# First attention with the values as the stationary operand, two heads side by side in TensorE's column halves

## The chip, the core and the metric

The kernel runs on one core of a Trainium2 chip. The metric is the device time of one execution in microseconds (us). The core has a matmul engine (TensorE, PE in the views, with its weight loads shown as PEld), a vector engine (VectorE, DVE), a scalar engine (ScalarE, ACT), GpSimd (POOL) and a DMA queue that SyncE (SP) fills. Each engine works through its own instructions in order and waits on semaphores that others raise.

## The reference

One decoder layer on x (512 tokens x 1024). A single input projection feeds two attention branches. Cut to what matters here:

```
h = x @ w_in; split into qa, ka, va, ga, iq, ik, iw, c_q, c_kv, k_rope, gb
# branch A: 8 heads of 64; a token indexer picks 128 keys for each query
att = qa . ka * 64**-0.5, where the key is picked and causal, else -inf
o_a = softmax(att) @ va                      # per head
# branch B: 8 heads, latent attention, keys of 64 + 32, values of 64, causal
o_b = softmax(...) @ vb
out = concat(o_a * silu(ga), o_b * silu(gb)) @ w_out
x   = layernorm(2**0.25 * x + out)
```

## The kernel before

The 512 tokens are four row tiles of 128. After the input projections (until about 172 us of the profiled execution), both attentions run in one loop over **units**. A unit is one row tile and one head; there are 32 of branch A (units 0 to 31) and 32 of branch B (32 to 63). Row tiles come in the order 3, 2, 1, 0 (`ORDER`), so that a unit has N = 512, 384, 256 or 128 keys (up to the diagonal), eight heads of each in a row.

The loop is software-pipelined by numbers written out by hand. At **step u** TensorE issues the scores of unit u (`scores`, two f32r matmuls into one of two PSUM banks), the transposes of unit u-2 (`transposes`, `T_LAG`; one per 128 keys, into one of two PSUM slots) and the outputs of unit u-4 (`outputs`, `PV_LAG`). In between, VectorE masks the scores and takes their minimum (`mask_unit`), ScalarE exponentiates with a row sum (`exp_unit`), and ScalarE copies the transposed probabilities from PSUM to SBUF (`copy_probsT`, a ring of three buffers). The scores of unit u wait for the mask of u-2, the transposes wait for the exponentials and for the copy of the slot two before, and the outputs wait for the copy.

In branch A's outputs (line 1369) the transposed probabilities (128 keys x 128 queries) are loaded as weights and the values stream, 64 columns. These are plain-f32 matmuls, which the trace shows as two records each: 80 matmuls, 160 records. When a row tile is through, VectorE divides by the row sums (`normalise`, 128x512 out of PSUM) and multiplies by the gate (`apply_gate`); TensorE transposes the result in four pieces (`o_transposes(i, 0)`), ScalarE rounds it out of PSUM (`copy_oT_hi`) and VectorE takes the remainder (`oT_low`) for the output projection (`out_products`, line 1425), which is spread over the steps of branch B.

GpSimd has, in its queue, the rounding of w_out (`wo_hi`, `wo_lo`; the last eight pieces at line 528), two low parts of branch B's values (line 522), and in branch B the merging of pairs (`merge_pair`) and the scaling of gates (`scale_gate`, line 504).

Of the kernel before, what the change touches and what calls it, by code (L numbers as in the profile page):

```python
# [6 lines left out]
P = 128  # L7
# [13 lines left out]
BANK = 512  # L21
# [6 lines left out]
def build(nc, x, xT, positions, freqs, w_in, q_norm_g, w_uq, kv_norm_g, w_ukv, w_out, ln_g, ln_b, out):  # L28
# [60 lines left out]

    def unit(u):  # L90
        v, h = divmod(u, HEADS)
        m = ORDER[v % TT]
        return v, m, h, (m + 1) * P


    O_AFTER = [[NU_A + HEADS * (i + 1) + OT_AT - T_LAG + b for b in range(2)] for i in range(TT - 1)] + [[NU, NU]]
    O_AFTER[0][0] = O_FIRST
# [48 lines left out]
    o_norm = sb("o_norm", 92, [P, A_WIDTH])  # L146
# [29 lines left out]
    probsT = sb("probsT", 26, [P, 3, BANK])  # L176
# [31 lines left out]
    neg_max, row_sum, rinv = col(8), col(NU), col(HEADS)  # L208
    stats, aggr, rstd = col(24), col(3), col(1)
    minus_half, unused = col(2 * TT), col(1)  # L210

    with ExitStack() as ctx:
# [40 lines left out]
        transposed, probsT_copied = sem("transposed"), sem("probsT_copied")  # L253
# [5 lines left out]
        o_ps_read, o_ready = sem("o_ps_read"), sem("o_ready")  # L259
# [60 lines left out]

        def pair_done(g):

            return NU_A + 2 * (g + 1)
# [13 lines left out]
        def oT_low(eng, i, b):  # L337

            dst = (oT0, oT1)[i % 2]
            eng.wait_ge(oT_hi_ready, 2 * i + b + 1)  # L340
            src = ps_pT[:, slot_of[i, b] % 2].rearrange("p (a b) -> p a b", a=4) if b == 0 else obT[:, :, :]
            eng.tensor_tensor(dst[:, 1, 4 * b:4 * b + 4, :], src, dst[:, 0, 4 * b:4 * b + 4, :],
                              ALU.subtract).then_inc(oT_lo_ready, 1)
# [92 lines left out]
        def _(pool):  # L436
# [83 lines left out]
            for j in (3, 2):  # L520
# [3 lines left out]
            for j in range(KT, 2 * KT):  # L524
                k = j // 2
                pool.wait_ge(raw_b_loaded[k - KT // 2], 16)
                pool.wait_ge(wo_hi_ready, 2 * WO_ORDER.index(k) + 2)
                pool.tensor_tensor(wo_lo(k, j % 2), wo_raw_b[:, k - KT // 2, j % 2], wo_hi[:, k, j % 2],
                                   ALU.subtract).then_inc(w_lo_ready, 1)
# [6 lines left out]
            for g in range(POOL_PAIRS, NPAIR):  # L536
                if g > 0 and g % 4 == 0:
                    oT_low(pool, g // 4 - 1, 1)
                merge_pair(pool, g)
                if g == 1:  # L540
# [15 lines left out]
        def _(act):  # L556
# [124 lines left out]
            def exp_unit(u):  # L681
# [3 lines left out]
                               scale=-1.0, accum_out=row_sum[:, u:u + 1]).then_inc(probs_ready, 1)  # L685
# [12 lines left out]
            def copy_probsT(u):  # L698
                N = unit(u)[3]
                act.wait_ge(transposed, slot_of[u] + 1)  # L700
                if u >= 3:
                    act.wait_ge(pv_done, u - 2)
                dst = probsT[:, u % 3, 0:N] if u < NU_A else probsT_b[:, u % 3, 0, 0:N]
                act.activation(dst, ps_pT[:, slot_of[u] % 2, 0:N], ACT.Copy).then_inc(probsT_copied, 1)  # L704

            def copy_oT_hi(i, b):
                n = slot_of[i, b]
# [4 lines left out]
                if b == 0:  # L712
                    act.wait_ge(transposed, n + 1)
                    src = ps_pT[:, n % 2].rearrange("p (a b) -> p a b", a=4)
# [3 lines left out]
                act.activation((oT0, oT1)[i % 2][:, 0, 4 * b:4 * b + 4, :], src, ACT.Copy).then_inc(oT_hi_ready, 1)  # L718

# [19 lines left out]
            for u in range(NU + T_LAG):  # L739
                if u >= T_LAG:  # L740
# [9 lines left out]
                if u == O_FIRST + T_LAG:  # L750
                    copy_oT_hi(0, 0)
                if 0 < i < TT and j == OT_AT + 2:
# [15 lines left out]
        def _(dve):  # L768
# [188 lines left out]
            def normalise(v):  # L957

                dve.wait_ge(pv_done, HEADS * (v + 1))
                after(V.reciprocal(rinv, row_sum[:, HEADS * v:HEADS * (v + 1)]))  # L960
                V.tensor_tensor(o_norm[:, :].rearrange("p (h d) -> p h d", h=HEADS),
                                ps_o[:, v % 2].rearrange("p (h d) -> p h d", h=HEADS),
                                rinv.unsqueeze(2).broadcast_to([P, HEADS, A_DIM]), ALU.mult).then_inc(o_ps_read, 1)

            def apply_gate(v):
                m = ORDER[v % TT]
                cols = slice(A_WIDTH * (v // TT), A_WIDTH * (v // TT + 1))
                dve.wait_ge(o_ps_read, v + 1)
                wait_tok(dve, G_GA, m)
                V.tensor_tensor(gate[:, m, cols], o_norm[:, :], gate[:, m, cols], ALU.mult).then_inc(o_ready, 1)  # L970

            def probs_low(u):
                N, w = unit(u)[3], u % 3
                dve.wait_ge(probsT_copied, u + 1)
# [73 lines left out]
            for u in range(NU):  # L1048
                if u >= 2:
                    mask_unit(u)  # L1050
                if u - T_LAG >= NU_A:
# [6 lines left out]
                if 0 < v <= TT and j == PV_LAG and v != TT - 1:  # L1058
                    normalise(v - 1)
                if 0 < v <= TT and j == PV_LAG + 1 and v != TT - 1:  # L1060
                    apply_gate(v - 1)
                if u == NU_A:
                    normalise(TT - 2)
                if u == NU_A + 2:
                    apply_gate(TT - 2)
# [4 lines left out]
                if u == O_FIRST + T_LAG + 1:  # L1070
                    oT_low(V, 0, 0)
# [39 lines left out]
        def _(pe):  # L1111
# [223 lines left out]
            def slot(n):  # L1335
# [3 lines left out]
                elif not isinstance(slots[n - 2], int):  # L1339
                    i, b = slots[n - 2]  # L1340
                    pe.wait_ge(*((oT_lo_ready, 2 * i + 1), (obT_ready, i + 1))[b])
                elif slots[n - 2] < NU_A:
                    pe.wait_ge(probsT_copied, slots[n - 2] + 1)
# [12 lines left out]
            def outputs(u):  # L1356
                v, m, h, N = unit(u)
                if v < TT:
                    if h == 0:
                        if v < 2:  # L1360
                            pe.wait_ge(acc_read[v], ACC_LAST[v])
                        else:
                            pe.wait_ge(o_ps_read, v - 1)
                        if v == 0:
                            for t in range(TT):
                                wait_tok(pe, G_V, t)
                    pe.wait_ge(probsT_copied, u + 1)
# [144 lines left out]
```

## Time and profile before

| | us |
|---|---|
| median of 3 runs | 301.69 (301.47 to 302.53) |
| the profiled execution | 301.67 |
| its span in the trace | 299.9 |
| TensorE busy | 291.2 (97%) |
| VectorE, ScalarE, GpSimd busy | 228.5, 165.6, 169.8 |
| branch A's outputs (line 1369), 160 records | 21.4 busy |
| granted TensorE clock, mean | 0.992 |

What ends outside the span is 1.8 us. A line of the timeline is: start and length in us, engine, line, operation, output <- inputs, shapes, count, and in brackets the idle time of the engine before it with what ended it. Records of TensorE overlap, since matmuls are pipelined: what one costs its engine is read from the distance between starts, not from its length. The same holds, to a smaller degree, for VectorE and ScalarE. Line numbers are those of the kernel before.

### The profile page before, as it was taken

The numbers are of one execution on the slowest core, as the hardware profiler recorded it, in microseconds if no ns is written. First come the engines' busy times: TensorE is split into PE (matmuls) and PEld (weight loads), VectorE is DVE, ScalarE is ACT, GpSimd is POOL, SyncE is SP. The second block draws the span as 40 slices with busy tenths as digits, with TensorE's granted clock in tenths as the row PEclk, the third lists the DMA queues.
The fourth block names the chain that finished last, engine by engine and source line by source line (L and its number), as shares of the span: only waits on it lengthen the run. The fifth ranks groups of instructions, "written<-read, shape, count | busy, mean of one in ns | idle before, by whom it ended". The sixth has DMA issues, their size and how long they took to land.

```text
span 299.9 us, 5192 instructions
## 1 busy us (share of the span) xinstructions
PE 291.2 (97%) x1664; PEld 248.6 (83%) x1664; DVE 228.5 (76%) x523; ACT 165.6 (55%) x397; POOL 169.8 (57%) x197
## 2 busy tenths in 40 slices
PE   8999999999999999999999999999999999999990
PEld 7999987778888888888888789998677788888890
DVE  2898689879999999994134663564898878977785
ACT  4754533692252272383267787888877786553200
POOL 5798965106999975445317697630594161817211
PEclk9999999999999999999999999999999999999996
DMA  7965552200533723220056577301940000030412
GB/s 230 354 183 179 144 149 75 67 0 0 154 96 102 207 76 105 70 72 0 0 149 143 211 203 156 125 2 43 359 161 3 0 0 2 36 106 3 140 70 72
DMA packets 19547, 31.86 MB, mean 106 GB/s; under 512 B 6496, under 2 KB 9056, under 8 KB 19520
## 3 DMA queue, kind: packets, MB, share of 16 engines
q1 hardware_dynamic: 19088, 31.35, 34.4%
q8 instruction: 14, 0.23, 0.3%
q10 hardware_dynamic: 432, 0.18, 0.3%
q14 instruction: 13, 0.11, 0.1%
HBM read 26.28 MB, written 2.10 MB: 95 GB/s over the span
## 4 chain that ended last, share of the span: by engine, by line
PE 93%; DVE 2%; DMA 1%; ACT 1%; issue 1%; DVEq 0%; ACTq 0%
PE ps L1117 50%; PE ps L1425 15%; PE ps L1353 6%; PE ps L1318 5%; PE ps L1369 5%; PE ps L1384 3%; PE ps L1308 2%; PE ps L1132 2%; PE ps L1311 2%; PE ps L1221 1%; DMA w_raw<-in_w_in 1%; PE ps L1242 1%; PE ps L1398 1%; DVE y_last L1031 0%; ACT probs L684 0%
## 5 line engine op out<-in xcount | busy, mean ns | idle before, releaser
L474 POOL TENSOR_TENSOR w_lo<-w_raw,w_hi 128x512 fp32r<-128x512 f32 (+3 forms) x62 | 79.3, 1301 | 34.0 <-ACT w_hi L573 33.8
L1117 PE MATMUL ps<-w_hi,x_lo 128*128 128x512 f32 (+2 forms) x224 | 82.6, 372 | 0.0
L1117 PE MATMUL ps<-w_lo,x_hi 128*128 128x512 f32 (+2 forms) x224 | 82.5, 371 | 0.0
L573 ACT ACTIVATE w_hi<-w_raw 128x512 fp32r<-128x512 f32 (+3 forms) x62 | 35.9, 590 | 68.9 <-PE ps L1117 61.8
L1117 PE MATMUL ps<-w_hi,x_hi 128*128 128x512 f32 (+1 forms) x188 | 73.6, 391 | 0.0
L1117 PEld LDWEIGHTS ps<-w_hi,x_lo 128*128 128x128 f32 x224 | 42.1, 188 | 6.5
L1117 PEld LDWEIGHTS ps<-w_lo,x_hi 128*128 128x128 f32 x224 | 42.2, 188 | 6.0
L1425 PE MATMUL ps<-wo_hi,oT 128*128 128x512 f32 (+1 forms) x144 | 43.5, 372 | 0.0
L1117 PEld LDWEIGHTS ps<-w_hi,x_hi 128*128 128x128 f32 x188 | 35.3, 188 | 7.1 <-ACT w_hi L573 0.7
L684 ACT ACTIVATE probs<-probs,small 128x512 f32<-128x512 f32 (+3 forms) x64 | 35.8, 559 | 7.6 <-DVE small L944 7.0
L1353 PE MATMUL ps<-ident,probs 128*128 128x128 f32 x160 | 28.3, 274 | 0.4 <-ACT probs L684 0.2
L1425 PEld LDWEIGHTS ps<-wo_hi,oT 128*128 128x128 f32 x144 | 25.7, 189 | 3.3
L1353 PEld LDWEIGHTS ps<-ident,probs 128*128 128x128 f32 x160 | 20.1, 140 | 9.5 <-issue 5.2
L332 POOL TENSOR_TENSOR obT<-half_sum,crossed 64x128 f32<-64x128 f32 x30 | 15.7, 522 | 17.8 <-ACT crossed L737 16.1
L901 DVE MATCH_REPLACE8 score<-small,score 128x256 f32<-128x256 f32 (+2 forms) x48 | 25.7, 554 | 0.0
L944 DVE CUSTOM_DVE_ANT_0 probs<-ps,score 128x512 f32<-128x512 f32 (+2 forms) x24 | 13.3, 556 | 15.1 <-PE ps L1311 15.1
L898 DVE MAX8 small<-score 128x8 f32<-128x256 f32 (+2 forms) x48 | 23.7, 556 | 0.0
L944 DVE CUSTOM_DVE_ANT_0 probs<-ps,causal 128x128 f32<-128x128 f32 (+3 forms) x40 | 17.8, 444 | 7.0 <-PE ps L1318 3.4
L1318 PE MATMUL ps<-kbT,qbT 96*128 96x512 f32 (+3 forms) x64 | 22.7, 435 | 0.0
L1369 PE MATMUL ps<-va,probsT 128*128 128x64 f32 x160 | 21.4, 264 | 0.0
L1369 PEld LDWEIGHTS ps<-va,probsT 128*128 128x128 f32 x160 | 20.5, 193 | 0.6 <-issue 0.6
L975 DVE TENSOR_TENSOR probsT_b<-ps,probsT_b 128x512 fp32r<-128x512 f32 (+3 forms) x32 | 15.6, 488 | 5.0 <-ACT probsT_b L704 4.7
(164 smaller groups left out, 548.5 us busy)
## 6 DMA issues: line engine op xcount, KB each, us to landing
w_raw<-in_w_in SPq DMA_DIRECT2D x20, 512.0 KB, 3.7
kaT_swap<-kaT SPq DMA_DIRECT2D x8, 256.0 KB, 3.7
w_raw<-in_w_out SPq DMA_DIRECT2D x4, 512.0 KB, 4.9
wo_early<-in_w_out SPq DMA_DIRECT2D x4, 512.0 KB, 5.3
wo_raw_b<-in_w_out SPq DMA_DIRECT2D x4, 512.0 KB, 5.6
x_res<-in_x SPq DMA_DIRECT2D x4, 512.0 KB, 6.6
x_raw<-in_xT SPq DMA_DIRECT2D x3, 512.0 KB, 6.9
out_y<-y SPq DMA_DIRECT2D x6, 256.0 KB, 2.1
```

The source lines that it names most:

```text
L332: eng.tensor_tensor(obT[rows, g % 4], half_sum[rows, g % 2, a], crossed[rows, g % 2], ALU.add).then_inc(pair_merged, 1)
L474: pool.tensor_tensor(w_lo[:, s, 0:n], w_raw[:, s, 0:n], w_hi[:, s, 0:n], ALU.subtract).then_inc(w_lo_ready, 1)
L573: act.activation(dst, w_raw[:, s, 0:n], ACT.Copy).then_inc(w_hi_ready, 1)
L684: act.activation(probs[:, u % NPROBS, 0:N], probs[:, u % NPROBS, 0:N], ACT.Exp, bias=neg_max[:, u % 8:u % 8 + 1], scale=-1.0, accum_out=ro ...
L898: step(V.max(top8[:, 8 * j:8 * j + 8], sc))
L901: step(V.match_replace(out=sc, in_to_replace=top8[:, 8 * j:8 * j + 8], in_values=sc, imm_value=TAKEN))
L944: V.tensor_tensor_reduce(out=probs[:, u % NPROBS, 0:N], in0=ps_s[:, u % 2, 0:N], in1=bias, scale=-scale, scalar=3.0e38, op0=ALU.add, op1=A ...
L1117: ins = mm(dst, a, b, start=start and j == 0, stop=stop and j == len(pairs) - 1)
L1318: ins = mm(ps_s[:, b, 0:N], qbT[:, h, t], kbT[:, h, 0:N], start=True, stop=True)
L1353: ins = nc.tensor.transpose(bank[:, j * P:(j + 1) * P], probs[:, u % NPROBS, j * P:(j + 1) * P], ident[:, :])
L1369: ins = mm(ps_o[:, v % 2, h * A_DIM:(h + 1) * A_DIM], probsT[:, u % 3, j * P:(j + 1) * P], va[:, j, h * A_DIM:(h + 1) * A_DIM], start=(j = ...
L1425: ins = mm(out_ps(i, b), oT[i % 2][:, o, k, :], w[:, wcols], start=first, stop=final)
```

## The change

Branch A's loop is changed in six ways; branch B's arithmetic stays.

1. **Order of units.** The row tiles of branch A come in two blocks, (3, 0) and (2, 1): `unit(u)` takes two heads of the long tile, two heads of the short tile, two more of the long, and so on. Key counts run 512, 512, 128, 128 four times, then 384, 384, 256, 256 four times.
2. **Outputs.** The values (128 keys x 64) are the weights, and the transposed probabilities stream, 128 columns. The even head of a pair writes PSUM partitions 0 to 63, the odd one 64 to 127. TensorE does them four units at a visit, at steps 7, 11, ... 35. The result stands transposed, heads on partitions, in four banks instead of two.
3. **Copies.** VectorE makes three of four copies of branch A's transposed probabilities, ScalarE the fourth (`by_dve`); the ring has five buffers.
4. **Gates.** GpSimd scales a tile's gate by the reciprocal row sums (`scale_gate_a`), TensorE transposes the gate instead of the result (after units 26, 28, 34 and 36), ScalarE copies it out (`turn_gate`) and VectorE multiplies (`gate_oaT`). `normalise` and `apply_gate` are gone.
5. **Output projection.** Its first half for row tile 3 begins at step 41 with three matmuls a step (before: step 34, two a step). The rounded copies of branch A's result come out of SBUF.
6. **GpSimd's queue** takes the first `oT_low` and the four gates, and two of the four late w_out pieces move behind merges of branch B.

```diff
+    BLOCKS = [(0, 3), (1, 2)]
     def unit(u):
-        v, h = divmod(u, HEADS)
+        if u < NU_A:
+            n, r = divmod(u, BLOCK_UNITS)
+            v, h = BLOCKS[n][r % 4 // 2], r // 4 * 2 + r % 2
...
+        def by_dve(u):
+            return u < NU_A and u % 4 != ACT_COPY
...
+        def copy_free(eng, u):
+            if u < NU_A:
+                if u >= len(probsT):
+                    eng.wait_ge(pv_done, u + 1 - len(probsT))
...
+            for v in BLOCKS[0]:
+                scale_gate_a(v)
+            vb_low_pool(3)
+            oT_low(pool, 0, 0)
+            vb_low_pool(2)
+            for v in BLOCKS[1]:
+                scale_gate_a(v)
+            for k in range(KT // 2, KT - 2):
+                wo_low_b(k)
...
+            def gate_oaT(v):
+                half = gate[:, ORDER[v], 0:A_WIDTH]
+                dve.wait_ge(gate_a_turned, A_RANK.index(v) + 1)
+                dve.wait_ge(pv_done, BLOCK_UNITS * (A_RANK.index(v) // 2 + 1))
+                V.tensor_tensor(half, oa_bank(v), half, ALU.mult).then_inc(o_ps_read, 1)
...
-                        ins = mm(ps_o[:, v % 2, h * A_DIM:(h + 1) * A_DIM], probsT[:, u % 3, j * P:(j + 1) * P],
-                                 va[:, j, h * A_DIM:(h + 1) * A_DIM], start=(j == 0), stop=(j == m))
+                    for w in (u - 3, u - 1):
...
+                        for j in range(m + 1):
+                            for a in range(2):
+                                ins = mm(oa_bank(v)[A_DIM * a:A_DIM * (a + 1), h // 2 * P:(h // 2 + 1) * P],
+                                         va[:, j, (h + a) * A_DIM:(h + a + 1) * A_DIM],
+                                         probsT[(w + a) % len(probsT)][:, j * P:(j + 1) * P], start=(j == 0), stop=(j == m))
...
-O_FIRST = 16
-A_HALF_AT = 34
+O_FIRST = 33
+TURN_AT = [26, 34, 36, 28]
+ACT_COPY = 3
+A_HALF_AT = 41
```

**TensorE, inside branch A.** The kernel before, one step of a unit with 512 keys (kaT and qaT are keys and queries, ident the identity of the transposes, va the values):

```order
L1308 MATMUL ps<-kaT,qaT 128x512 [waits masked_ready]
L1311 MATMUL ps<-kaT_swap,qaT 128x512
L1353 MATMUL ps<-ident,probs 128x128 [waits probs_ready,probsT_copied]
L1353 MATMUL ps<-ident,probs 128x128 x3
L1369 MATMUL ps<-va,probsT 128x64 [waits probsT_copied]
L1369 MATMUL ps<-va,probsT 128x64 x3
```

The kernel after, from the second long unit of a group (step 9) to the beginning of the visit (step 11):

```order
L1384 MATMUL ps<-kaT_swap,qaT 128x512
L1426 MATMUL ps<-ident,probs 128x128 [waits probs_ready,probsT_copied_dve]
L1381 MATMUL ps<-kaT,qaT 128x128 [waits masked_ready]
L1384 MATMUL ps<-kaT_swap,qaT 128x128
L1426 MATMUL ps<-ident,probs 128x128 [waits probs_ready,probsT_copied_dve]
L1426 MATMUL ps<-ident,probs 128x128 x3
L1381 MATMUL ps<-kaT,qaT 128x128 [waits masked_ready]
L1384 MATMUL ps<-kaT_swap,qaT 128x128
L1426 MATMUL ps<-ident,probs 128x128 [waits probs_ready,probsT_copied]
L1426 MATMUL ps<-ident,probs 128x128 x3
L1447 MATMUL ps<-probsT_105,va 64x128 [waits probsT_copied_dve]
L1447 MATMUL ps<-probsT_101,va 64x128
```

Between the scores of a unit and its transposes there stood two steps' outputs; now there stand only scores and transposes, and the outputs of four units (ten matmuls, two heads in turn) come in one piece behind the fourth step.

**VectorE, inside branch A.** The kernel before, around the end of the first row tile (`ISA` rows are the masks and the reads of their minimum):

```order
L944 ISA probs,small<-ps,score 128x384 [waits transposed,scores_ready]
L944 ISA small 128x1
L960 RECIPROCAL small<-small 128x8 [waits pv_done]
L961 TENSOR_TENSOR o_norm<-ps,small 128x512 [waits dve_step]
L944 ISA probs,small<-ps,score 128x384 [waits transposed,scores_ready]
L944 ISA small 128x1
L970 TENSOR_TENSOR gate<-o_norm,gate 128x512 [waits acc_read3,o_ps_read]
```

The kernel after, steps 12 to 15:

```order
L1017 ISA probs,small<-ps,score 128x512 [waits transposed,scores_ready]
L1017 ISA small 128x1
L1032 COPY probsT_101<-ps 128x128 [waits pv_done,transposed]
L1017 ISA probs,small<-ps,score 128x512 [waits transposed,scores_ready]
L1017 ISA small 128x1
L1017 ISA probs,small<-ps,causal 128x128 [waits transposed,scores_ready]
L1017 ISA small 128x1
L1032 COPY probsT_103<-ps 128x512 [waits pv_done,transposed]
L1017 ISA probs,small<-ps,causal 128x128 [waits transposed,scores_ready]
L1017 ISA small 128x1
L1032 COPY probsT_104<-ps 128x512 [waits pv_done,transposed]
```

The two wide operations for each row tile are gone from between the masks, and a copy stands behind three of four masks.

**GpSimd, around the end of branch A.** The kernel before, from its last early piece of w_out on (vb_parts are branch B's values, wo_lo_b the late pieces, obT the merged pairs):

```order
L519 TENSOR_TENSOR wo_lo_a<-w_raw,wo_hi 128x512
L522 TENSOR_TENSOR vb_parts_98<-vb,vb_parts_98 128x4x128 [waits vb_hi_ready]
L522 TENSOR_TENSOR vb_parts_97<-vb,vb_parts_97 128x4x128 [waits vb_hi_ready]
L528 TENSOR_TENSOR wo_lo_b<-wo_raw_b,wo_hi 128x512 [waits wo_hi_ready,raw_b_loaded0] x2
L528 TENSOR_TENSOR wo_lo_b<-wo_raw_b,wo_hi 128x512 [waits wo_hi_ready,raw_b_loaded1] x2
```

The kernel after:

```order
L563 TENSOR_TENSOR wo_lo_a<-w_raw,wo_hi 128x512
L571 TENSOR_TENSOR gate<-gate,small 128x512 [waits acc_read3,rinv_a_ready]
L571 TENSOR_TENSOR gate<-gate,small 128x512 [waits acc_read0,rinv_a_ready]
L576 TENSOR_TENSOR vb_parts_97<-vb,vb_parts_97 128x4x128 [waits vb_hi_ready]
L386 TENSOR_TENSOR oT_68<-gate,oT_68 128x512 [waits oT_hi_ready]
L576 TENSOR_TENSOR vb_parts_96<-vb,vb_parts_96 128x4x128 [waits vb_hi_ready]
L571 TENSOR_TENSOR gate<-gate,small 128x512 [waits acc_read2,rinv_a_ready]
L571 TENSOR_TENSOR gate<-gate,small 128x512 [waits acc_read1,rinv_a_ready]
L584 TENSOR_TENSOR wo_lo_b<-wo_raw_b,wo_hi 128x512 [waits wo_hi_ready,raw_b_loaded0]
```

Four gates and one `oT_low` have come in; the second values piece, for which branch B's first outputs wait, stands behind the `oT_low`, and that waits for ScalarE's copy at step 33.

## Rows read from the trace of the kernel before

**Rows 1.** Windows view: us, busy PE, PEld, DVE, ACT, POOL (instructions), clock, DMA share, GB/s.
```profile
core 0 of [0], span 299.9 us
...
172.00:208.00 36.00, 35.76 (x296) 33.99 (x295) 19.22 (x71) 29.92 (x92) 21.01 (x25) 1.00 0.38 101
```

**Rows 2.** TensorE in time (start, length in us): one unit of 512 keys.
```profile
175.86 0.48 PE L1308 MATMUL ps<-kaT,qaT 128*128 128x512 f32 x1
...
176.41 0.60 PE L1353 MATMUL ps<-ident,probs 128*128 128x128 f32 x4
...
176.85 1.00 PE L1369 MATMUL ps<-va,probsT 128*128 128x64 f32 x8
...
177.66 0.48 PE L1308 MATMUL ps<-kaT,qaT 128*128 128x512 f32 x1
```

**Rows 3.** TensorE in time: starts of units with 384, 256 and 128 keys.
```profile
191.81 0.42 PE L1308 MATMUL ps<-kaT,qaT 128*128 128x384 f32 x1
...
193.17 0.36 PE L1308 MATMUL ps<-kaT,qaT 128*128 128x256 f32 x1
...
199.52 0.36 PE L1308 MATMUL ps<-kaT,qaT 128*128 128x256 f32 x1
...
200.42 0.37 PE L1308 MATMUL ps<-kaT,qaT 128*128 128x256 f32 x1
...
206.03 0.31 PE L1308 MATMUL ps<-kaT,qaT 128*128 128x128 f32 x1
...
206.57 0.30 PE L1308 MATMUL ps<-kaT,qaT 128*128 128x128 f32 x1
```

**Rows 4.** TensorE in time: plain-f32 scores of second attention, then transposes.
```profile
216.65 1.02 PE L1318 MATMUL ps<-kbT,qbT 96*128 96x512 f32 x2
...
217.51 0.60 PE L1353 MATMUL ps<-ident,probs 128*128 128x128 f32 x4
```

**Rows 5.** TensorE in time: matmuls in four strips of 32 rows.
```profile
59.99 0.50 PE L1221 MATMUL ps<-ik_hi,iq_hi 32*128 32x512 f32 x4
...
60.56 0.40 PE L1221 MATMUL ps<-ik_hi,iq_lo 32*128 32x512 f32 x4
...
60.89 0.50 PE L1117 MATMUL ps<-w_hi,x_hi 128*128 128x512 f32 x1
```

**Rows 6.** Timeline: from unit 2's scores to its transposes, four engines.
```profile
172.05 0.39 PE L1308 MATMUL ps<-kaT,qaT 128*128 128x512 f32 x1
...
172.71 0.69 DVE L944 CUSTOM_DVE_ANT_0 probs<-ps,score 128x512 f32<-128x512 f32 x1 [2.45 <-PE ps L1311]
...
173.64 0.71 ACT L684 ACTIVATE probs<-probs,small 128x512 f32<-128x512 f32 x1
...
174.56 0.42 PEld L1353 LDWEIGHTS ps<-ident,probs 128*128 128x128 f32 x4 [0.52 <-issue]
```

**Rows 7.** VectorE in time: a mask of 512 keys and the operation behind it.
```profile
220.42 0.68 DVE L944 CUSTOM_DVE_ANT_0 probs<-ps,causal 128x512 f32<-128x512 f32 x1
221.03 0.08 DVE L944 DVE_READ_ACCUMULATOR2_ANT small<- 128x1 f32 x1
```

**Rows 8.** Groups by line and shape (busy us, mean ns | idle before).
```profile
L1369 PEld LDWEIGHTS ps<-va,probsT 128*128 128x128 f32 x160 | 20.5, 193 | 0.6 <-issue 0.6
...
L684 ACT ACTIVATE probs<-probs,small 128x384 f32<-128x384 f32 x16 | 9.8, 610 | 1.1 <-DVE small L944 1.0
...
L944 DVE CUSTOM_DVE_ANT_0 probs<-ps,causal 128x128 f32<-128x128 f32 x16 | 4.6, 286 | 4.0 <-PE ps L1311 3.3 <-PE ps L1318 0.5
```

**Rows 9.** GpSimd in time: pieces of its queue around the second attention.
```profile
213.24 1.29 POOL L522 TENSOR_TENSOR vb_parts<-vb,vb_parts 128x512 fp32r<-128x512 f32 x1 [11.03 <-ACT vb_parts L728]
...
214.49 10.93 POOL L528 TENSOR_TENSOR wo_lo_b<-wo_raw_b,wo_hi 128x512 fp32r<-128x512 f32 x8
...
230.01 1.05 POOL L504 TENSOR_TENSOR gate<-gate,small 128x512 f32<-128x512 f32 x1 [0.88 <-POOL obT L332]
```

**Rows 10.** Weight loads in time: a wait inside the first attention.
```profile
198.87 0.20 PEld L1353 LDWEIGHTS ps<-ident,probs 128*128 128x128 f32 x2 [0.31 <-DVE oT L342]
```

More of the change, by code:

```diff
@@ L88, in build, with sum_col @@
     NPAIR = TT * B_HEADS // 2
+    BLOCKS = [(0, 3), (1, 2)]
+    A_RANK = [v for block in BLOCKS for v in block]
+    BLOCK_UNITS = 2 * HEADS
     def unit(u):
-        v, h = divmod(u, HEADS)
+        if u < NU_A:
+            n, r = divmod(u, BLOCK_UNITS)
+            v, h = BLOCKS[n][r % 4 // 2], r // 4 * 2 + r % 2
+        else:
+            v, h = divmod(u, HEADS)
         m = ORDER[v % TT]
         return v, m, h, (m + 1) * P
-    O_AFTER = [[NU_A + HEADS * (i + 1) + OT_AT - T_LAG + b for b in range(2)] for i in range(TT - 1)] + [[NU, NU]]
-    O_AFTER[0][0] = O_FIRST
+    def sum_col(u):
+        v, m, h, N = unit(u)
+        return HEADS * (A_RANK.index(v) if v < TT else v) + h
+    O_AFTER = [[TURN_AT[i], NU_A + HEADS * (i + 1) + OT_AT - T_LAG + 1 if i < TT - 1 else NU] for i in range(TT)]
     slots = []
@@ L319, in out_ps, with wait_copied, oaT, oa_bank @@
             return bank[:, 0:PIECES[i][b].stop - PIECES[i][b].start]
+        def by_dve(u):
+            return u < NU_A and u % 4 != ACT_COPY
+        def wait_copied(eng, u):
+            n = sum(by_dve(w) for w in range(u + 1))
+            if by_dve(u):
+                eng.wait_ge(probsT_copied_dve, n)
+            else:
+                eng.wait_ge(probsT_copied, u + 1 - n)
+        def copy_free(eng, u):
+            if u < NU_A:
+                if u >= len(probsT):
+                    eng.wait_ge(pv_done, u + 1 - len(probsT))
+                return probsT[u % len(probsT)][:, 0:unit(u)[3]]
+            if u >= NU_A + 3:
+                eng.wait_ge(pv_done, u - 2)
+            return probsT_b[:, u % 3, 0, 0:unit(u)[3]]
+        def oaT(i):
+            return gate[:, ORDER[i], 0:A_WIDTH].rearrange("p (a b) -> p a b", a=4)
+        def oa_bank(v):
+            return (ps_o, ps_y)[A_RANK.index(v) // 2][:, A_RANK.index(v) % 2]
         def pair_done(g):
@@ L340, in oT_low @@
             eng.wait_ge(oT_hi_ready, 2 * i + b + 1)
-            src = ps_pT[:, slot_of[i, b] % 2].rearrange("p (a b) -> p a b", a=4) if b == 0 else obT[:, :, :]
+            src = oaT(i) if b == 0 else obT[:, :, :]
             eng.tensor_tensor(dst[:, 1, 4 * b:4 * b + 4, :], src, dst[:, 0, 4 * b:4 * b + 4, :],
@@ L539, in _ @@
                 merge_pair(pool, g)
+                if g <= 2:
+                    wo_low_b(KT - 3 + g)
                 if g == 1:
@@ L739, in _ @@
             for u in range(NU + T_LAG):
-                if u >= T_LAG:
+                if u >= T_LAG and not by_dve(u - T_LAG):
                     copy_probsT(u - T_LAG)
@@ L1050, in _ @@
                     mask_unit(u)
+                if u >= T_LAG and by_dve(u - T_LAG):
+                    copy_probsT(u - T_LAG)
                 if u - T_LAG >= NU_A:
@@ L1057, in _ @@
                 i = v - TT
[L1058 to L1065, printed above, removed]
+                if u in (BLOCK_UNITS + 2, NU_A + 2):
+                    row_sums_a(u // BLOCK_UNITS - 1)
+                if u - T_LAG - 2 in TURN_AT:
+                    gate_oaT(TURN_AT.index(u - T_LAG - 2))
                 if v > TT and j == 2:
@@ L1439, in _ @@
                 i, j = divmod(u - NU_A, HEADS)
[L1440 to L1445 removed]
+                for t in range(TT):
+                    if u == O_AFTER[t][0] + T_LAG:
+                        o_transposes(t, 0)
+                if 0 < i < TT and j == OT_AT + 1:
+                    o_transposes(i - 1, 1)
+                if 0 <= u - A_HALF_AT < 8:
+                    out_products(0, 3 * (u - A_HALF_AT), 3 * (u - A_HALF_AT + 1))
                 if 0 <= u - OUT_AT[0] - 2 < 6:
@@ L1452, in _ @@
             out_products(TT - 2, done, NSTEP - LAST_STEPS)
-            for b in range(2):
-                o_transposes(TT - 1, b)
+            o_transposes(TT - 1, 1)
             out_products(TT - 2, NSTEP - LAST_STEPS, NSTEP)
```

109 lines of the change are left out of this document (55 added, 54 removed).

## Prediction

> **What bounds the kernel now.** I read the windows view first. In the stretch of branch A, 172 to 208 us, TensorE is busy 35.76 of 36.00 us, VectorE 19.2, ScalarE 29.9, GpSimd 21.0 [rows 1]. So the matmuls set the pace, and what leaves TensorE there shortens the run, as long as nothing else comes up behind it. Next the timeline of TensorE. A unit of 512 keys takes 1.80 us: 0.55 from the first score matmul to the transposes, 0.44 for four transposes (0.11 each), 0.81 for eight records of outputs, 0.10 each [rows 2]. Units of 384, 256 and 128 keys take 1.36, 0.90 and 0.54 [rows 3]; less 0.11 for each transpose and 0.10 for each output record, that leaves 0.43, 0.28 and 0.23 for their scores. All 160 output records cost 16.1 us. The third thing to read is latency, at the one place where the trace shows it bare. Units 2 and 3 run before any outputs: scores at 172.05, mask at 172.71, exponentials at 173.64, transposes only at 174.56, and TensorE sat there ("issue", 0.52) [rows 6]. From scores to transposes are 2.5 us, against two steps of 1.8 us with outputs. **The outputs that the change shortens are what covers this chain.**
>
> **Part 1, the outputs.** A record now streams 128 columns. The nearest price is the plain-f32 scores of branch B: two records of 512 columns take 0.86 us, 0.107 for 128 columns [rows 4]. A visit has 20 records, in both blocks (4+1 or 3+2 key tiles, two heads, two records). If the halves overlap fully, a visit is 10 x 0.107 and one more stream until the second half is through, 1.18; if they don't, 20 x 0.107 = 2.14. That matmuls in separate parts of the array run together the trace shows for strips of rows only: three groups of four matmuls with 512 columns (the rows have the first and the third) take their turns from 59.99 to 60.89, 0.075 us each, where even 128 columns need 0.107 alone [rows 4, 5]. Leaving the strips cost at most 0.1: 0.33 from the last group to the next matmul, where the groups stand 0.285 apart [rows 5]. Behind the outputs the change to f32r matmuls costs 0.1 already today (below) and stands inside the 0.55. I take 1.2 for a visit, bounds 1.1 and 1.4. Eight visits are 9.6 us against 16.1: **-6.5**, bounds -7.3 and -4.9.
>
> The Trainium skill, "TensorEngine Tiling (Array Packing)", Key Properties, says that a change of tiling mode drains TensorE. With the 0.1 of rows 5 on either side a visit would be 1.4, which is the upper bound, and the sum 1.6 us worse; no run here shows it for columns yet.
>
> **Part 2, the chain.** One visit of the first block in steady state, from the moment t = 0 at which the scores of the long unit a begin. Constants: a result of TensorE is seen 0.20 after its last matmul's turn (172.05 to 172.71, and 0.10 more behind outputs, make 0.75 to the mask) [rows 2, 6]. A mask of 512 occupies VectorE for 0.61 [rows 7], one of 128 for about 0.22 (286 ns less the same overlap) [rows 8]; exponentials begin 0.73 after the mask (its 0.69 and a hand-over of 0.04, my estimate), occupy 0.71, and transposes come 0.95 after their start (0.92 to the weight load) [rows 6]. A copy by VectorE I take like a mask. TensorE:
> scores a 0 to 0.55, a short unit's transpose to 0.66, scores b to 1.21, a transpose to 1.32. Scores c wait until mask a is through and read, 0.75 + 0.61 + 0.13 = 1.49, and end at 1.72. Transposes of a: mask 0.75, exponentials 1.48, so 2.43; **wait 0.71**; end 2.87. Scores d to 3.10. Transposes of b: VectorE has mask a until 1.36, the copy of a short unit until 1.58, then mask b; exponentials at 2.38 (ScalarE has a until 2.19 and one copy), so 3.33; wait 0.23; end 3.77. Visit: 4.97. The old kernel needs 2 x 1.80 + 2 x 0.54 = 4.68 for the same units. The waits are 0.17 + 0.71 + 0.23 = **1.1**.
>
> The second block the same way, with 0.43, 0.28, masks 0.48 and 0.35 (between the two known), exponentials 0.61 [rows 8] and so transposes 0.85 after their start: scores c need no wait; a's transposes at 0.63 + 0.60 + 0.85 = 2.08 against 1.58, wait 0.5; b's wait 0.2. Together **0.7**.
>
> Sum of waits over the stage: the first group (steps 4 to 7) I take at 2.0, twice a steady one, since VectorE also has four transposes of branch B's queries there; two groups of the first block 2.2; three groups of the second 2.1; the last group has two gate transposes (4 x 0.11 each) in its holes, 0. That is 6.3. The old kernel has 0.52 and 0.31 of its own [rows 6, 10]. **Net +5.5**, bounds +3.5 and +7 (a tenth more or less in the hand-over in each link).
>
> **Part 3, what moves without much cost.** Sixteen gate transposes replace sixteen result transposes: nothing. VectorE loses 8 wide operations and gains 24 copies, 4 `gate_oaT` and 2 small reciprocals: per group of the first block masks 1.66 and copies 1.42, 3.1 us of 4.97, so it isn't the bound; what it costs is in the chain. ScalarE loses 24 copies and gains four. Three gate transposes leave places amid f32r matmuls, where each cost a change of kind, 3 x 0.1: **-0.3**. The output matmuls that move from steps 34-40 to 41-48 keep their number; the steps that they leave have TensorE work of some 1.8 us (0.86 + 0.44 + outputs), and VectorE about as much.
>
> **Part 4, GpSimd's queue.** At step 36 TensorE needs the second values piece for branch B's first outputs and the scaled gate of tile 2. Both stand behind the new `oT_low`, which waits for ScalarE's copy at step 33: from there 1.3 (the piece, and `oT_low` alike) + 1.29 + 1.05 = 3.6 us [rows 9]. By the steps' sizes TensorE gets there 3.1 to 3.6 us after that copy, so it waits up to 0.6, and 0.3 at the transposes of step 35, whose exponentials stand behind two value copies. I take **+0.7**, bounds 0 and +2. SyncE's loads of w_out are released by the scores of step 31, at nearly the same time.
>
> **Sum.** -6.5 + 5.5 - 0.3 + 0.7 = -0.6 us on the profiled execution's 301.67, which is the median's 301.69 to within 0.02: **301.1 us**. Its own range, with a visit and the chain at their bounds but not all at once, is 298.5 to 303.5.
>
> **Rivals.**
> *The chain doesn't bind.* If masks and exponentials come earlier than in my walk, the whole saving stays: -6.5 - 0.3 = -6.8, 294.9. For it: TensorE showed under 1 us of waits in 36 us. Against it: rows 6 show the 2.5 us bare, and steps without outputs are exactly what the change makes.
> *The column halves don't overlap.* Place: the visit. Price: 2.14 and two changes of mode, 2.3 instead of 1.2, 8 x 1.1 = +8.8: 309.9, slower. It decides from the point where a visit takes more than about 1.3 us. For it: no row shows column halves. Against it: rows 5, for strips of rows.
> The Trainium skill, "TensorE: Matmul & The Clock Gate", The mechanism, says that weight loads overlap matmuls in flight only when the row groups differ, and column halves share all rows. Taken at its word a visit would be near 4 us and the run 20 us slower. The trace disagrees for the whole array: output records 0.10 apart have loads of 0.19 on the same rows [rows 2, 8]. So I give it little of this rival's chance.
> *GpSimd is late for good.* Two late pieces of w_out (10.93 / 4 = 2.7 each) stand between merges of pairs, and behind the merges are VectorE's pair reads and the gating of `obT`. If its queue reaches branch B some 5 us late, TensorE waits at step 46 for one piece and a gate, 2.7 + 1.05 [rows 9]: +3.8 on the forecast, 304.9. Against it: it idled 11 us before the second values piece.
>
> **Chances.** Forecast 0.58 (of it faster by over half a per cent 0.22, within 0.30, slower 0.06); chain doesn't bind 0.16, all faster; halves don't overlap 0.14, slower; GpSimd late 0.12 (0.03 within, 0.09 slower). Half a per cent, 1.5 us, is about what a measurement can tell from no change. So faster 0.38, same 0.33, slower 0.29. The range, 294.0 to 306.5, leaves out the non-overlapping halves and about a third of the first rival.
>
> **What the profile after would show.** The visit: ten output matmuls in about 1.2 us; 2.1 or more refutes overlap. The chain: TensorE waiting in the first block about 0.7 before a's transposes, released by the exponentials, and VectorE near 60% in the stage; no wait there refutes the walk. GpSimd: the wait at step 36, and none at 46. The stage should still end near 208 us. I would be wrong above all if the waits come out at half or double.

## The result

| | us |
|---|---|
| before, median of 4 runs | 301.88 (301.47 to 302.53) |
| after, median of 4 runs | 308.16 (307.93 to 309.57) |
| ratio of the two | 1.0216, 95% interval 1.018 to 1.0252 |
| forecast | 301.1 (294.0 to 306.5) |

The changed kernel is slower, by 6.3 us, and outside the range. The profiled execution of after was the slowest of the four. A second profile of the same kernel, taken in the experiments, gave 307.81, so the comparison of places uses that one; the difference between the two profiles comes at the end. The busy times come first, from the page of that second profile:

```profile
PE 289.5 (95%) x1664; PEld 240.6 (79%) x1664; DVE 234.3 (77%) x540; ACT 157.7 (52%) x377; POOL 173.4 (57%) x202
```

TensorE's records cover 1.7 us less than before (289.5 against 291.2), while the span grew by 6.1 (306.0 against 299.9), so it isn't work that was added. These are TensorE's own waits from 172 us on, by what ended them, in the second profile of after (us in total, times, longest):

```profile
PE ps L1426 <- ACT probs L752: 3.8, 9, 0.6
PE ps L1426 <- ACT gate L789: 3.4, 3, 1.6
PE ps L1381 <- DVE small L1017: 0.6, 1, 0.6
PE ps L1478 <- POOL gate L571: 0.2, 1, 0.2
```

The kernel before has one wait of 0.2 us in this list; its two bare places inside branch A, 0.5 and 0.3, show in the weight loads [rows 6, 10]. Now three sorts of waits stand in it: for the exponentials (line 752), which the prediction walked; once for a mask (line 1381); and **3.4 us for ScalarE's copies of transposed gates (line 789)**, which it did not have at all. The 0.2 for a scaled gate (line 571) was forecast. Over 172 to 208 us the stage reads so now, against 35.76 busy before [rows 1]:

```profile
172.00:208.00 36.00, 30.05 (x257) 23.27 (x255) 24.34 (x84) 20.47 (x69) 22.34 (x27) 1.00 0.38 102
```

A steady group of the first block on TensorE, from the scores of one long unit to those of the next group. Read the starts; the idle time is in brackets:

```profile
184.56 0.51 PE L1381 MATMUL ps<-kaT,qaT 128*128 128x512 f32 x1
...
185.16 0.47 PE L1381 MATMUL ps<-kaT,qaT 128*128 128x512 f32 x1
...
186.09 0.33 PE L1381 MATMUL ps<-kaT,qaT 128*128 128x128 f32 x1
...
187.03 0.63 PE L1426 MATMUL ps<-ident,probs 128*128 128x128 f32 x4 [0.50 <-ACT probs L752]
...
187.90 0.63 PE L1426 MATMUL ps<-ident,probs 128*128 128x128 f32 x4
188.46 1.31 PE L1447 MATMUL ps<-probsT,va 128*64 128x128 f32 x20
189.70 0.45 PE L1381 MATMUL ps<-kaT,qaT 128*128 128x384 f32 x1
```

Up to the visit it is the walk of Part 2 to a few hundredths. From the first scores at 184.56 the scores of the short unit come at 1.53 (walked: 1.49), a's transposes at 2.47 with a wait of 0.50 (2.43, 0.71), b's at 3.34 (3.33). Then the visit: it was to begin at 3.77 and begins at 3.90, and it takes 1.24 us for its 20 records, so that the group is 5.14 long against 4.97 forecast. The halves do overlap: 0.062 us a record, against 0.107 for 128 columns alone [rows 4].

And this is the mechanism that the prediction missed, in time, on TensorE, VectorE and ScalarE (gate L1478 is the transpose of a gate, L789 its copy out of PSUM):

```profile
204.79 0.60 PE L1478 MATMUL ps<-ident,gate 128*128 128x128 f32 x4
...
206.13 0.28 PE L1384 MATMUL ps<-kaT_swap,qaT 128*128 128x256 f32 x1
...
206.26 0.08 DVE L1017 DVE_READ_ACCUMULATOR2_ANT small<- 128x1 f32 x1
...
206.49 0.61 ACT L752 ACTIVATE probs<-probs,small 128x384 f32<-128x384 f32 x1
...
207.08 0.59 ACT L789 ACTIVATE gate<-ps 128x512 f32<-128x512 f32 x1
...
207.72 0.55 PE L1426 MATMUL ps<-ident,probs 128*128 128x128 f32 x3 [1.31 <-ACT gate L789]
```

TensorE transposes the first gate at 204.79. Transposed probabilities and transposed gates share two PSUM slots, and the transposes of the unit two places later (unit 28, line 1426) need the gate's slot. ScalarE copies it out only at 207.08, since `turn_gate` stands in its queue one step later, behind the exponential of unit 29 (206.49), whose mask VectorE had read only at 206.34. TensorE is through with its scores of unit 30 (from 206.13) and stands for 1.31 us. The same happens twice more in branch B, where the list of waits has otherwise only 0.28 us for an exponential and 0.19 for a scaled gate:

```profile
223.43 0.66 PE L1426 MATMUL ps<-ident,probs 128*128 128x128 f32 x4 [0.54 <-ACT gate L789]
...
228.98 0.66 PE L1426 MATMUL ps<-ident,probs 128*128 128x128 f32 x4 [1.55 <-ACT gate L789]
```

### The profile page after: what moved, and what is told of

Same layout as the page of the kernel before. It is cut to its first block, busy times and chain, and to the rows that moved or that the text cites. A ratio compares the mean times of both kernels' runs of the same rounds, so it can differ in the third digit from the quotient of the medians.

```text
span 307.7 us, 5205 instructions
## 1 busy us (share of the span) xinstructions
PE 291.2 (95%) x1664; PEld 241.8 (79%) x1664; DVE 233.6 (76%) x540; ACT 157.8 (51%) x377; POOL 174.1 (57%) x202
## 4 chain that ended last, share of the span: by engine, by line
PE 89%; ACT 4%; issue 3%; DVE 2%; POOL 1%; DVEq 0%; POOLq 0%; ACTq 0%
PE ps L1190 49%; PE ps L1505 14%; PE ps L1426 6%; PE ps L1391 4%; PE ps L1447 3%; PE ps L1464 3%; PE ps L1205 2%; ACT probs L752 2%; PE ps L1336 1%; PE ps L1294 1%; PE ps L1478 1%; PE ps L1381 1%; PE ps L1315 1%; PE ps L1384 1%; ACT gate L789 0%
## 5 line engine op out<-in xcount | busy, mean ns | idle before, releaser
L1426 PE MATMUL ps<-ident,probs 128*128 128x128 f32 x160 | 29.2, 281 | 7.4 <-ACT probs L752 3.7
L1032 DVE COPY probsT<-ps 128x512 f32<-128x512 f32 (+3 forms) x24 | 12.8, 534 | 11.9 <-PE ps L1447 8.1
L770 ACT ACTIVATE probsT_b<-ps 128x512 fp32r<-128x512 f32 (+3 forms) x32 | 13.8, 430 | 14.1 <-PE ps L1426 14.0
L1464 PE MATMUL ps<-probsT_b,vb_parts 128*128 128x256 f32 x80 | 17.2, 312 | 0.0
```

The lines of the kernel that those rows point to most:

```text
L1426: ins = nc.tensor.transpose(bank[:, j * P:(j + 1) * P], probs[:, u % NPROBS, j * P:(j + 1) * P], ident[:, :])
L1464: ins = mm(ps_o[:, g % 2, 2 * P * a:2 * P * (a + 1)], vb_parts[j][:, h // 2, 2 * a:2 * a + 2].rearrange("p a d -> p (a d)"), probsT_b[:, u ...
```

## The experiments

Ratios refer to the kernel before, run on the same chip (301.8 to 302.0 us in each series). Differences to "after" refer to its median of 308.16, which comes from another series and is known to about 1.1 us either way (the interval of its ratio), so differences of less than that between such gains say little. Theory A: the late gate copies hold a transpose slot, and this costs about 3.4 us. Theory B: the bare chain of mask, exponential and transposes costs the rest, and a visit placed where it covers the chain gets it back. The rival: one of them is only the visible end of the other, so that undoing it exposes the other and the gain is shared.

### Gate copies one step earlier

```diff
-                if u - T_LAG - 1 in TURN_AT:
-                    turn_gate(TURN_AT.index(u - T_LAG - 1))
+                if u - T_LAG in TURN_AT:
+                    turn_gate(TURN_AT.index(u - T_LAG))
```

> Only ScalarE's queue is changed: the copy of a transposed gate stands one step earlier, behind the exponentials of step 28, 30, 36, 38 instead of 29, 31, 37, 39. Theory A (the gate's PSUM slot is held until ScalarE has copied it, and that copy stands behind an exponential that waits for a mask): the waits of 1.31, 0.54 and 1.55 us that end with that copy in the trace go, 3.4 us, 304.8. Rival (the transposes there would wait for their exponentials anyway): under 1 us, 307.2 or more.

Measured: 304.05 us (303.74 to 304.85), ratio 1.0086 (1.0065 to 1.0106). One place in ScalarE's queue is worth 4.1 us, give or take the 1.1 of after. Its waits:

```profile
PE ps L1426 <- ACT probs L752: 3.7, 9, 0.6
...
PE ps L1426 <- ACT gate L789: 0.2, 1, 0.2
```

3.4 us of gate waits have become 0.2, and the exponentials' waits, 3.8 before, are 3.7: they did not take the place of the others. The rows account for 3.2 of the 4.1. Theory A stands.

### The visit ahead of the next group's short scores

```diff
             for u in range(NU + PV_LAG):
+                if u % 4 == 2 and 6 <= u <= NU_A + 2:
+                    outputs(u - 3)
                 if 2 <= u < NU:
                     scores(u)
...
-                if u - PV_LAG >= 0:
+                if u - PV_LAG >= NU_A:
                     outputs(u - PV_LAG)
```

> The visit of four units' outputs stands ahead of the scores of the short unit c (step 4k+2) instead of behind the transposes of step 4k+3; nothing else. Theory B (TensorE waits in each group because nothing covers the chain from scores to transposes, and the visit can cover it): a group of the first block falls from 5.13 to about 4.0 us, one of the second from 4.57 to about 3.9, so 6 to 7 us over the stage, 301.5. Rival (VectorE or ScalarE is the bound in the stage, so that the place of the visit doesn't matter): groups stay near 5.1 and 4.6, under 1 us.

Measured: 304.55 us (304.14 to 306.04), ratio 1.0094 (1.0073 to 1.0115): 3.6 us faster than after, 3.1 short of what theory B gave. The gate copies were not touched and still cost 2.7 us of waits. What is new is 1.7 us of waits for ScalarE's copy of probabilities, which the next run shows in time.

### Both

> Both edits. If the two kinds of wait are separate, the gains add: 298.1 by theories A and B. If they share a chain, it is nearer to 300.5.

Measured: 301.94 us (301.44 to 302.76), ratio 1.0007 (0.9995 to 1.0019), as fast as the kernel before, and slower than both expectations: A and B together fall short. The waits for exponentials and masks are gone from the matmuls' list; in their place stands one line, which had 1.7 us in the run before:

```profile
PE ps L1447 <- ACT probsT L770: 2.6, 5, 0.9
```

```profile
184.69 1.09 PE L1447 MATMUL ps<-probsT,va 128*64 128x128 f32 x16
186.13 0.44 PE L1447 MATMUL ps<-probsT,va 128*64 128x128 f32 x4 [0.35 <-ACT probsT L770]
186.50 0.33 PE L1381 MATMUL ps<-kaT,qaT 128*128 128x128 f32 x1
```

The long pair's 16 records begin at 184.69, and the 4 of the short pair wait until 186.13 for ScalarE's copy of the fourth unit (line 770), which that engine makes behind an exponential. The next scores stand behind them. The visit was brought forward to cover a wait and ran into its own input. The separate gains, 4.1 and 3.6, make 7.7, and both edits together give 6.2. The 1.5 that is missing is hardly more than the noise of after, but 0.9 of it shows in the trace: with the gate waits gone, the wait for ScalarE's copy grows from 1.7 to 2.6. With the whole visit in this place part of the gain is shared, as the rival has it.

### The two heads of a pair one after the other

```diff
-                        for j in range(m + 1):
-                            for a in range(2):
+                        for a in range(2):
+                            for j in range(m + 1):
```

> The changed kernel with the two heads of a pair one after the other (all key tiles of the even head, then of the odd one) in place of in turn. If the two column halves overlap only where neighbours in the queue are in different halves, a visit goes from 1.24 us to 20 x 0.107 = 2.1, and the run by 8 x 0.9 = 7 us, 315. If the 1.24 us came from smaller weights alone, nothing changes.

Measured: 312.02 us (one run). A visit of the first block (4 + 1 key tiles) and one of the second (3 + 2):

```profile
185.26 1.80 PE L1447 MATMUL ps<-probsT,va 128*64 128x128 f32 x20
186.99 0.50 PE L1381 MATMUL ps<-kaT,qaT 128*128 128x512 f32 x1
...
201.60 1.58 PE L1447 MATMUL ps<-probsT,va 128*64 128x128 f32 x20
203.12 0.44 PE L1381 MATMUL ps<-kaT,qaT 128*128 128x384 f32 x1
```

Three visits take 1.73 us and four take 1.51, instead of 1.24 or 1.25, so these seven cost 2.5 us more. The first visit took 3.24 us, at a lowered clock (last column but two):

```profile
178.00:180.00 2.00, 2.00 (x16) 1.93 (x16) 0.26 (x3) 0.49 (x2) 2.00 (x3) 0.52 0.80 283
180.00:182.00 2.00, 2.00 (x14) 1.54 (x11) 0.69 (x1) 0.00 (x0) 1.92 (x3) 0.63 1.14 269
```

The only run of this kernel is thus to be set beside the execution of after that has the same (309.57, see the last experiment), and is 2.5 us slower than it, not the 3.9 that after's median gives; with one execution of each this is a rough figure. So the alternation of halves does make them overlap, but the heads one after the other are still below 20 x 0.107 = 2.14 us, and the loss is under half of the one expected. Matmuls at the joints between heads still have neighbours in the other half; since both kinds of visit have three joints and take 1.73 and 1.51, joints alone don't explain it. Why the rest overlaps stays open.

### The visit cut in two

Against the run of both edits; `outputs` has got the second argument:

```diff
                 if u % 4 == 2 and 6 <= u <= NU_A + 2:
-                    outputs(u - 3)
+                    outputs(u - 3, (0,))
                 if 2 <= u < NU:
                     scores(u)
                 if 0 <= u - T_LAG < NU:
                     transposes(u - T_LAG)
+                if u % 4 == 2 and 6 <= u <= NU_A + 2:
+                    outputs(u - 3, (1,))
```

Here (0,) is the long pair and (1,) the short one; the gate copies are a step earlier too.

> Both moves again (gate copies one step earlier on ScalarE, outputs of a group brought forward), but the visit is cut in two: the long pair stands ahead of the scores of step 4k+2 as before, the short pair behind the transposes of that step, so that the scores of a unit of the next group no longer queue behind ScalarE's copy of the last short unit. Theory C (with both moves in, what is left is the visit's wait for that copy: five waits for it, 2.6 us together, in the run of both moves): those waits go and about 2.5 us are won, 299.4 us, faster than the kernel before. Rival D (VectorE's turn of mask and copy bounds the group: ten waits of 0.3 us for its copies, each before transposes): the waits for ScalarE's copy are only exchanged for longer waits for VectorE's, less than 0.8 us is won, 301.2 us or more.

Measured: **298.88 us (298.63 to 298.94), ratio 0.9899 (0.9884 to 0.9913)**. It beats both kernels: 1.0% under the one before, 9.3 us under the changed one. All that is left in the list of the matmuls' waits, and the stage:

```profile
PE ps L1478 <- POOL gate L571: 0.2, 1, 0.2
```

```profile
172.00:208.00 36.00, 35.71 (x307) 26.82 (x306) 28.65 (x96) 24.00 (x77) 22.40 (x27) 1.00 0.45 125
```

35.71 us busy of 36: TensorE sets the pace again [rows 1]. A group of the first block, on TensorE:

```profile
178.04 0.48 PE L1381 MATMUL ps<-kaT,qaT 128*128 128x512 f32 x1
...
179.37 1.09 PE L1447 MATMUL ps<-probsT,va 128*64 128x128 f32 x16
180.39 0.33 PE L1381 MATMUL ps<-kaT,qaT 128*128 128x128 f32 x1
...
180.67 0.62 PE L1426 MATMUL ps<-ident,probs 128*128 128x128 f32 x4
181.22 0.44 PE L1447 MATMUL ps<-probsT,va 128*64 128x128 f32 x4
181.59 0.33 PE L1381 MATMUL ps<-kaT,qaT 128*128 128x128 f32 x1
...
182.25 0.48 PE L1381 MATMUL ps<-kaT,qaT 128*128 128x512 f32 x1
```

4.21 us (178.04 to 182.25) against 5.14 in after and 4.68 for the same units before. The long pair takes 1.02 us, the short one 0.37, together 0.15 more than a whole visit. Theory C held: the waits for ScalarE's copy are gone, and 3.1 us were won.

Of rival D something is left, where the list of matmul waits doesn't show it. A group of the second block, matmuls and weight loads:

```profile
190.50 0.42 PE L1381 MATMUL ps<-kaT,qaT 128*128 128x384 f32 x1
...
191.06 0.42 PE L1381 MATMUL ps<-kaT,qaT 128*128 128x384 f32 x1
...
191.63 0.20 PEld L1426 LDWEIGHTS ps<-ident,probs 128*128 128x128 f32 x2 [0.29 <-DVE probsT L1032]
...
192.08 0.66 PEld L1447 LDWEIGHTS ps<-probsT,va 128*64 128x64 f32 x12 [0.25 <-issue]
192.11 0.88 PE L1447 MATMUL ps<-probsT,va 128*64 128x128 f32 x12
192.91 0.39 PE L1381 MATMUL ps<-kaT,qaT 128*128 128x256 f32 x1
...
193.68 0.66 PE L1447 MATMUL ps<-probsT,va 128*64 128x128 f32 x8
...
194.27 0.39 PE L1381 MATMUL ps<-kaT,qaT 128*128 128x256 f32 x1
```

The weight loads stand 0.29 us for VectorE's copy, and the step from 191.06 to 192.11 takes 1.05 us for work that the prediction's prices put at 0.65. The ends of matmul records are modelled, so a short wait can hide between them. This group takes 4.36 us (to 194.86) and the next one 4.26, against 4.52 for the same units before. So the second block gains about 0.2 us a group, the first 0.5.

The parts of visits also show what a visit is made of: 4, 8, 12 and 16 records take 0.37, 0.59, 0.80 and 1.02 us and a whole visit of 20 takes 1.24, which is 0.15 and 0.054 for each record.

### The cut visit without the earlier gate copies

The edits of the visit stay; ScalarE's queue is the changed kernel's again.

```diff
-                if u - T_LAG in TURN_AT:
-                    turn_gate(TURN_AT.index(u - T_LAG))
+                if u - T_LAG - 1 in TURN_AT:
+                    turn_gate(TURN_AT.index(u - T_LAG - 1))
```

> The outputs brought forward and cut in two as in e7_split, but the gate copies left one step later on ScalarE, as in the changed kernel. Theory A (a gate transpose holds one of two transpose slots until ScalarE's copy, and this price is paid wherever the visits stand): the waits for the gate copies are back at steps 28, 38 and 40, and the time is 298.9 + 4 = 302.9 us. If the gate copies only cost while the chain of mask and exponential is bare as well, one of the three waits goes and the time is 300.5 us.

Measured: 302.18 us (301.89 to 302.99), ratio 1.0012 (1.0003 to 1.0022).

```profile
PE ps L1426 <- ACT gate L789: 2.9, 4, 1.6
```

With the chain covered the gate waits are all there, four of them now, 2.9 us, and the run costs 3.3 us more than with the copies a step earlier. So the four runs form a square: after 308.16, gate copies alone -4.1, cut visit alone -6.0, both -9.3. The 0.8 us by which the sum of the two differs from both together is within the noise of after, so with the cut visit the two causes are independent as far as these runs can tell, and the rival (one hides the other) falls for it. With the whole visit, above, part of the gain was shared.

### The whole visit behind the transposes, or between scores and transposes

Both with the earlier gate copies; `outputs(u - 3)` stands at step 4k+2, in the first run behind `transposes` (below), in the second between `scores` and `transposes`.

```diff
                 if 0 <= u - T_LAG < NU:
                     transposes(u - T_LAG)
-                if u - PV_LAG >= 0:
+                if u % 4 == 2 and 6 <= u <= NU_A + 2:
+                    outputs(u - 3)
+                if u - PV_LAG >= NU_A:
                     outputs(u - PV_LAG)
```

> Gate copies one step earlier, and the whole visit of four heads moved from step 4k+3 to step 4k+2, but behind the transposes of that step, so nothing covers the time from the first unit's mask to its transposes. If what the forward move of the visit won came from covering that chain, the wait of 0.5 us before the first long unit's transposes stays in each group and the time is near that of the earlier gate copies alone, 304.0 us. If it came from the visit lying a step earlier at all (copies released earlier), it is near 302.0 us.

Measured: 302.54 us (301.94 to 303.04), ratio 1.0021 (1.0012 to 1.0031), between the two expectations and nearer to the second.

```profile
PE ps L1426 <- ACT probs L752: 2.5, 6, 0.5
PE ps L1381 <- DVE small L1017: 1.1, 3, 0.6
```

> Gate copies one step earlier; the visit whole again, between the scores and the transposes of step 4k+2. By the rows of e7_split its two parts take TensorE 1.02 + 0.37 us against 1.24 for a whole visit, so one visit saves 0.15 x 8 = 1.2 us of work. Against that the scores of the short unit lose the long pair that stood ahead of them and wait for VectorE's mask of the first long unit (0.23 us in a steady group, 0.61 in the first, as in e9_behind), some 0.4 us a group with the copy of the last short unit: 8 x 0.4 - 1.2 = +2, 300.9 us. Rival: the visit covers whatever follows it, so that the place before or behind these scores doesn't matter, and the saved work is all gain: 297.7 us.

Measured: 300.63 us (300.17 to 301.19), ratio 0.996 (0.9947 to 0.9972), 0.3 from what was expected.

```profile
PE ps L1381 <- DVE small L1017: 1.2, 3, 0.6
```

Behind the transposes the visit covers nothing of the chain, and 2.5 us of waits for exponentials stay, though a step's advance alone won 1.5 us (the wait of 0.63 us at unit 21, below, is gone there). So of the 5.2 us between the gate copies alone and the cut visit (304.05 to 298.88), 1.5 come from the advance and only the other 3.7 from where within the step the outputs stand: theory B holds for the larger part. Between scores and transposes those waits are gone and the wait for the mask stays, 1.2 us in matmuls. Only ahead of both, with the part that isn't ready left for later, the matmuls have none of these waits.

### The changed kernel again

> The changed kernel unaltered, a second profile. If the 2.3 us of the first visit (178.7 to 181.0 us, at a granted clock of 0.5) is a matter of that one execution, the visit takes 1.25 us here, the span is 1.5 us shorter, 306.2, and the gate waits at steps 28, 38 and 40 (1.3, 0.5 and 1.5 us) are all there again. If short waits of TensorE lower the clock each time, the row with 0.5 is there again and the span is 307.7.

Measured: 307.81 us, span 306.0. The clock (last column but two) in the first profile of after, then in the second:

```profile
178.00:180.00 2.00, 2.00 (x16) 1.67 (x16) 0.45 (x3) 0.49 (x2) 2.00 (x3) 0.50 0.95 307
180.00:182.00 2.00, 2.00 (x17) 1.50 (x14) 0.88 (x2) 0.00 (x0) 1.92 (x4) 0.75 1.09 280
```

```profile
178.00:180.00 2.00, 2.00 (x25) 1.52 (x24) 1.00 (x4) 0.49 (x2) 2.00 (x3) 1.00 0.94 289
180.00:182.00 2.00, 1.39 (x8) 0.88 (x7) 1.79 (x8) 1.06 (x4) 1.92 (x3) 1.00 1.10 279
```

The granted clock was 0.50 for 2 us, that is the lower of its two levels, and 0.75 as a mean of the next 2, in one execution and full in the other, with waits of the same length ahead of it (0.61, 0.50 and 0.35 us). The first visit took 2.33 us at the lowered clock. The run of the two heads one after the other has the same waits and fell too (0.52 and 0.63), the run of the gate copies alone has them and did not; both ran on the same chip. The two profiles of after are 0.1 us apart at 172.3 us and 1.6 at the end of that visit, so the clock explains 1.5 of the 1.7 us of span between them, and nothing of the 6.3 between the kernels' medians.

## Where the prediction went wrong

By its own steps, against the second profile of after (span 306.0, before 299.9: +6.1, forecast -0.6).

- **Part 2, the walk: right.** 5.14 against 4.97, the waits in the forecast places. VectorE's share in the stage (24.34 of 36 us, 68%) came out above the 60% I named, and it is still not the bound.
- **Part 2, the last group, "two gate transposes in its holes, 0": wrong, and the main failure.** The gate transposes have a price that isn't TensorE's time: they hold a slot until another engine's queue gets to them. I followed them on TensorE alone, and in Part 3 set them equal to the old result transposes ("nothing"). The cost is 1.31 us at unit 28, and 0.54 and 1.55 in branch B at steps 38 and 40, where I had looked for no waits: **3.4 us in rows, 4.1 by the experiment**, which is the same within after's noise. For ScalarE I had only counted copies ("loses 24 copies and gains four"); behind what in its queue each of the four stands I did not ask.
- **Part 1, the visit: overlap right, size low.** A visit takes 1.24 us, but before its first weight load and before the first one behind it the loads stand still for 0.17 each:

```profile
183.32 1.07 PEld L1447 LDWEIGHTS ps<-probsT,va 128*64 128x64 f32 x20 [0.17 <-DVE probsT L1032]
184.56 0.19 PEld L1381 LDWEIGHTS ps<-kaT,qaT 128*128 128x128 f32 x1 [0.17 <-issue]
```

  The second stop lies within the 1.24. The first lies ahead of it: the four transposes before the visit take 0.56 to its start (187.90 to 188.46), where four cost 0.44. So a visit costs 1.24 + 0.13 = 1.37 against 1.2: 8 x 0.17 = **1.4 us**. I had 1.4 for a visit as the upper bound and did not take it. The Trainium skill, "TensorEngine Tiling (Array Packing)", Key Properties, says that a change of tiling mode drains TensorE. The trace agrees, by the 0.15 us that a part of a visit costs whatever its length and the 0.13 ahead of it, and the sum by that rule was the better one. The idle loads alone would not show it: stops of 0.18 stand in the kernel before too, which has no column halves (line 1353 at 224.01).
- **Part 2, second block: ScalarE's rounding of branch B's values** (`vb_high(0)`, 0.61 us) stands at step 20 ahead of the next exponential, and the transposes of unit 21 wait 0.63 us, where the other groups' have no wait: **+0.6**. Argued from the timeline, not tested by itself; in the cut version TensorE has no such wait. The last group is another **0.4** longer than its work, its visit and the 1.31; the trace shows weight loads that wait there for VectorE's copies (0.31 at 205.73, 0.18 at 208.92), none for exponentials.
- **Part 4: right.** 0.28 us for an exponential at step 35 and 0.19 for the scaled gate at step 36, together 0.5 against 0.7, and none at step 46: **-0.2**.
- **The sum.** 3.4 + 1.4 + 0.6 + 0.4 - 0.2 = 5.6 of the 6.7 us between forecast and measurement. About 1 us isn't assigned to any row. By the last item of this list it lies behind branch A's stage, and no row shows the -0.3 that Part 3 took for gate transposes.
- **The rivals.** None of the three came. The one that ends on the slow side ("halves don't overlap") was refuted by 1.24 us. The second rule weighed there, that weight loads overlap only when the row groups differ (the Trainium skill, "TensorE: Matmul & The Clock Gate", The mechanism), would have made a visit near 4 us; the trace disagrees, with 20 loads and 20 matmuls in 1.24 us. The first rival's 294.9 was out of reach even without the waits: the cut version, with the chain covered, gains 3.0 us and not 6.8. The visits' size takes 1.4 of the difference, cutting them 8 x 0.15 = 1.2; the stops for VectorE's copies in the second block are in the rest.
- **"The stage should still end near 208":** it ended at 210.64. The walk's own groups, added up from the first long scores at 173.40, end at 207.1 and not at 208; the 3.6 beyond that are the first gate wait (1.31), seven visits (1.2), the rounding (0.6) and the last group (0.4).

What would have found it: listing for each of the two PSUM slots who fills it, who empties it, and behind what the emptying stands.

## What to carry to other kernels

Where several producers share a small ring of PSUM banks, a new tenant costs the time until it is emptied, counted in the emptying engine's queue; move that copy as early as its data allows before judging the change. When outputs get shorter, what they covered becomes bare: cut them into pieces and put each piece where its inputs are just ready and the chain is still running, which here turned 2% slower into 1% faster than before. A walk through one period predicted its length to 0.17 us in 5.14, but only for the work that is in it every time; the exceptions (gates, a rounding of values) need a walk of their own. And a list of matmul waits without entries doesn't mean that TensorE never stands: look at the weight loads' waits and at the distance between starts too.

## What the runs showed of the hardware

- Plain-f32 matmuls of 128 columns that alternate between two column halves cost 0.054 us a record and 0.15 once for each run of them (0.37, 0.59, 0.80, 1.02 and 1.24 us for 4, 8, 12, 16 and 20 records). Alone a record costs 0.107 [rows 4]. With the heads one after the other, 20 records took 1.73 us (4 + 1 key tiles) and 1.51 (3 + 2).
- On entering and leaving the column halves the weight loads stop for 0.17 us. Cutting a visit in two cost 0.15 us within it (1.02 + 0.37 against 1.24), and 0.11 ahead of the second part (180.67 to 181.22, 0.55 us for four transposes of 0.11).
- After waits of TensorE of 0.61, 0.50 and 0.35 us within 3 us the granted clock fell to half in two profiled executions and not in two others.
